# Turning the convolved channels token-major: transposes on TensorE in place of block transposes on VectorE and moves on ScalarE

## The reference

```python
xbc_act, conv_new = causal_conv(xbc, conv_prev, conv_w, conv_b)      # silu inside
xs, bm, cm = jnp.split(xbc_act, [SSD_WIDTH, SSD_WIDTH + SSD_GROUPS * SSD_STATE], axis=-1)
...
xdt = xr * dtr[..., None]
cb = jnp.einsum("bclgn,bcsgn->bcgls", cm, bm)
y_diag = jnp.einsum("bcgls,bcgrls,bcsgrp->bclgrp", cb, decay, xdt)
chunk_states = jnp.einsum("bcsgn,bcgrs,bcsgrp->bcgrpn", bm, decay_to_end, xdt)
...
y = y + xh.astype(jnp.float32) * d_skip.astype(jnp.float32)[:, None]
```

## Time and profile before

| | |
|---|---|
| median of 3 runs | 2809.83 us (2806.76 to 2810.88) |
| the profiled execution | 2810.88 us |
| its span, first to last instruction | 2809.1 us |
| mean granted TensorE clock | 0.992 |
| TensorE busy | 2760.9 us (98%) |
| VectorE busy | 1768.2 us (63%) |
| ScalarE busy | 1252.3 us (45%) |
| GpSimd busy | 824.4 us (29%) |

### The profile page before, as it was taken

The page is one execution under the profiler, slowest core; times in us unless marked ns, Lnnn a source line. Parts: engine busy times, 40 slices in busy tenths (PEclk is TensorE's granted clock), DMA queues, the critical chain, the costliest instruction groups (busy, mean ns, idle before and its releaser), DMA issues.

```text
span 2809.1 us, 38015 instructions
## 1 busy us (share of the span) xinstructions
PE 2760.9 (98%) x11971; PEld 1794.1 (64%) x11971; DVE 1768.2 (63%) x4770; ACT 1252.3 (45%) x2692; POOL 824.4 (29%) x1368
## 2 busy tenths in 40 slices
PE   8999999999999999999999999997999999999997
PEld 6776777777776777677777776773444444444443
DVE  5756666665666565656665656565666666666665
ACT  2334333343334333433343334334666666666665
POOL 1121112111211121111111121112556565555555
PEclk9999999999999999999999999998999999999999
DMA  7311111111111111111111111156888687778864
GB/s 309 146 46 53 61 68 46 53 61 68 46 49 65 67 47 46 68 54 61 46 63 58 61 46 56 38 195 226 317 296 293 233 277 252 280 266 286 316 218 146
DMA packets 104908, 377.88 MB, mean 135 GB/s; under 512 B 32713, under 2 KB 34642, under 8 KB 94706
## 3 DMA queue, kind: packets, MB, share of 16 engines
q1 hardware_dynamic: 44226, 236.13, 22.9%
q0 software_dynamic: 60480, 139.24, 14.7%
HBM read 326.14 MB, written 123.03 MB: 160 GB/s over the span
## 4 chain that ended last, share of the span: by engine, by line
PE 96%; DMA 2%; DVE 1%; ACT 1%; issue 1%; SPq 0%; POOL 0%; DVEq 0%; POOLq 0%; ACTq 0%
PE PB L367 25%; PE PB L1629 20%; PE PB L378 16%; PE PB L456 12%; PE SS L1648 5%; PE TB L1648 5%; PE YB L456 4%; PE YB L411 2%; PE TB L356 1%; DMA arena<-in_w_in 1%; PE SS L420 1%; PE TB L433 1%; PE SS L424 1%; PE YB L1639 1%; PE MB L402 1%
## 5 line engine op out<-in xcount | busy, mean ns | idle before, releaser
L367 PE MATMUL PB<-arena,hT 128*128 128x512 f32 (+2 forms) x2112 | 725.0, 496 | 1.5 <-ACT xT L590 0.8
L1629 PE MATMUL PB<-arena,hT 128*128 x1296 | 582.5, 592 | 0.0
L367 PEld LDWEIGHTS PB<-arena,hT 128*128 128x128 f32 x2112 | 396.8, 191 | 269.6 <-issue 222.6
L378 PE MATMUL PB<-hT,arena 128*128 128x128 f32 x4224 | 487.3, 276 | 3.7 <-DVE arena L1118 3.7
L378 PEld LDWEIGHTS PB<-hT,arena 128*128 128x128 f32 x4224 | 481.7, 193 | 7.8 <-issue 4.0
L1629 PEld LDWEIGHTS PB<-arena,hT 128*128 128x128 f32 x1296 | 239.9, 190 | 271.2 <-issue 271.2
L1155 POOL TENSOR_SCALAR rs<-sq 128x2 f32<-128x2 f32 (+1 forms) x66 | 14.2, 215 | 1284.4 <-ACT h L739 938.6
L456 PE MATMUL PB<-arena,tT 128*128 128x274 f32 (+1 forms) x1056 | 359.4, 495 | 0.7 <-ACT tT L634 0.7
L456 PEld LDWEIGHTS PB<-arena,tT 128*128 128x128 f32 x1056 | 196.1, 191 | 141.8 <-issue 121.5
L812 DVE SCALAR_TENSOR_TENSOR xc<-xT,cols,xc 128x128 f32<-128x128 f32 x792 | 216.8, 347 | 3.5
L1759 DVE TENSOR_TENSOR gv<-ycat,PB 128x256 f32<-128x256 f32 x81 | 34.1, 421 | 291.9 <-ACT ycat L1711 276.0
(11 more groups left out here) (288 smaller groups left out, 3990.0 us busy)
## 6 DMA issues: line engine op xcount, KB each, us to landing
arena<-in_w_expert SPq DMA_DIRECT2D x32, 2048.0 KB
arena<-in_w_expert SPq DMA_DIRECT2D x32, 1024.0 KB
h_rows<-h SPq DMA_DIRECT2D x34, 512.0 KB, 2.8
x_in<-in_x_rows SPq DMA_DIRECT2D x33, 512.0 KB, 4.4
hT<-in_x_cols SPq DMA_DIRECT2D x33, 512.0 KB, 3.5
x_res<-in_x_rows SPq DMA_DIRECT2D x33, 512.0 KB, 4.2
dec<-running_sums SPq DMA_DIRECT2D x33, 512.0 KB, 3.6
x_rows<-x_res SPq DMA_DIRECT2D x33, 512.0 KB, 2.6
```

Of the source, the lines that this page charges most:

```text
L367: mm = nc.tensor.matmul(out, hT[u][:, k, :], w_group(name)[:, k, :], start=k == 0, stop=k == KD - 1)
L378: mm = nc.tensor.matmul(PB[b][:, c * P:(c + 1) * P], w_block(name, c)[:, k, :], hT[u][:, k, :], start=k == 0, stop=k == KD - 1)
L1629: mm = nc.tensor.matmul(PB[u][:, :], hT[u][:, k, :], arena[:, bass.ds(slot + k * 2 * DE, 2 * DE)], start=k == 0, stop=k == KD - 1)
```

## The change

`xtok` and `btok` become two tensors. After projection z TensorE transposes the four x blocks into `TB[0]` and the two B blocks into `TB[1]`, and ScalarE copies both from there, between the SiLU of z and the exponentials. ScalarE's twelve moves and VectorE's six transposes go. The users of `TB` get waits on the new copies, `xb_out`, which now counts two per tile.

```diff
--- before.py
+++ after.py
@@ -181,8 +181,8 @@
         xT = [m[:, 0:CB * (P + HALO)].rearrange("p (b t) -> p b t", b=CB) for m in xT_mem]
         xT_s = xT_mem[0][:, :].rearrange("p (b q l) -> p b q l", b=CB, q=SB)
         xc = sb("xc", [P, CB, P])
-        xbtok = sb("xbtok", [P, W + G * N])
-        xtok, btok = xbtok[:, 0:W], xbtok[:, W:]
+        xtok = sb("xtok", [P, W])
+        btok = sb("btok", [P, G * N])
         gu = sb("gu", [P, W])
         zz = sb("zz", [P, W])
         gv2 = sb("gv2", [P, 2, W])
@@ -258,7 +258,7 @@
 
         names = """tail_packed xa_scaled w_scaled eout_a ws_ready wow_full wow_out xsq_ready xr_ready xi_ready rbc_full x_scaled
             proj_xa proj_xb proj_va proj_vb proj_u proj_z xa_out xb_evicted va_out gv_out gu_out z_out cache_set
-            halo_saved conv_done xc_ready cb_done xc_moved xb_out
+            halo_saved conv_done xc_ready cb_done xb_full xb_out
             dt_read lg_read cb_read rank_read dtneg_ready dtexp_ready dtrec_ready dt_ready acs_out sumT_done sumT_out
             ein_ready eout_ready seg_done decay_ready dec_ready xw_ready
             mixed_done bn_ready vr_ready v_ready ycat_hi
@@ -397,6 +397,11 @@
         def pe_front_channels(pe, t):
 
             pe.wait_ge(s["xc_ready"], t + 1)
+            after(pe, s["ycT_out"], 2 * t)
+            for b in range(2):
+                for k in range(4 - 2 * b):
+                    mm = nc.tensor.transpose(TB[b][:, k, :], xc[:, 4 * b + k, :], ident)
+                mm.then_inc(s["xb_full"], 1)
             pe.wait_ge(s["acs_out"], t + 1)
             for g in range(G):
                 mm = nc.tensor.matmul(cb_p[:, g * P:(g + 1) * P], xc[:, 4 + g, :], xc[:, 6 + g, :], start=True, stop=True)
@@ -427,6 +432,7 @@
         def pe_mix_pair(pe, i):
 
             pe.wait_ge(s["v_ready"], i + 2)
+            pe.wait_ge(s["xb_out"], 2 * i + 2)
             if i == 0:
                 pe.wait_ge(s["ws_ready"], 1)
             for h in range(H):
@@ -436,7 +442,7 @@
         def pe_mix_sample(pe):
 
             pe.wait_ge(s["v_ready"], NT)
-            pe.wait_ge(s["ycat_hi"], NP)
+            pe.wait_ge(s["xb_out"], 2 * NP + 1)
             pe.wait_ge(s["ws_ready"], 2)
             for h in range(H):
                 mm = nc.tensor.matmul(flat(TB[0][:, :, :])[:, h * HD:(h + 1) * HD], wsT_s[:, h, :], gv[0][:, h * HD:(h + 1) * HD],
@@ -446,7 +452,7 @@
         def pe_turned(pe, i):
 
             pe.wait_ge(s["ycat_ready"], i + 1)
-            transpose8(pe, block_of(ycat), lambda b: [("ycat_hi", i + 1)], "ycT_full")
+            transpose8(pe, block_of(ycat), lambda b: [("ycat_hi", i + 1)] if b == 0 else [("xb_out", 2 * i + 2)], "ycT_full")
 
         def pe_out(pe, i, b, free):
 
@@ -503,7 +509,7 @@
                 pe.wait_ge(s["w_scaled"], len(W_COLS))
             pe_out(pe, i, 0, (s["gu_out"], i + 2))
             if tn.next2:
-                pe_spread(pe, i + 2, TB[0], [("ycat_hi", i + 1)])
+                pe_spread(pe, i + 2, TB[0], [("xb_out", 2 * i + 3)])
             pe_out(pe, i, 1, (s["z_out"], i + 2))
             pe_out(pe, i, 2, (s["gated_ready"], i + 1))
 
@@ -578,8 +584,6 @@
 
 
 
-        channels_moved = [tmp[:, 0:192], tmp[:, 192:384], ycat[:, 0:192]]
-
         def act_channels(act, b, t, u, to_sample, done):
 
             if to_sample:
@@ -633,31 +637,22 @@
                 after(act, s["out2"], i)
                 nc.scalar.activation(tT[:, half(b), :], TB[b][:, :, :], ACT.Copy).then_inc(s["ycT_out"], 1)
 
-        def channels_quarter(g, q):
-            return xc[32 * g:32 * (g + 1), 0:6, 32 * q:32 * (q + 1)]
-
-        def act_move_channels(act, t):
-
-            act.wait_ge(s["xc_ready"], t + 1)
-            if t > 0:
-                act.wait_ge(s["ycat_hi"], t)
-                act.wait_ge(s["ycT_out"], 2 * t - 1)
-            for g in range(3):
-                for q in range(4):
-                    ins = nc.scalar.activation(channels_moved[g][32 * q:32 * (q + 1), :], channels_quarter(g, q), ACT.Copy)
-            ins.then_inc(s["xc_moved"], 1)
-
         def act_silu(act, t):
 
             act.wait_ge(s["conv_done"], t + 1)
             nc.scalar.activation(xc[:, :, :], xc[:, :, :], ACT.Silu).then_inc(s["xc_ready"], 1)
-            act_move_channels(act, t)
             act.wait_ge(s["proj_z"], t + 1)
             after(act, s["gated_ready"], t)
             nc.scalar.activation(zz[:, :], PB[1][:, :], ACT.Silu).then_inc(s["z_out"], 1)
 
         def act_front(act, t):
 
+            act.wait_ge(s["xb_full"], 2 * t + 1)
+            after(act, s["gated_ready"], t)
+            nc.scalar.activation(xtok[:, :], flat(TB[0][:, :, :]), ACT.Copy).then_inc(s["xb_out"], 1)
+            act.wait_ge(s["xb_full"], 2 * t + 2)
+            after(act, s["states_done"], t)
+            nc.scalar.activation(btok[:, :], flat(TB[1][:, 0:2, :]), ACT.Copy).then_inc(s["xb_out"], 1)
             act.wait_ge(s["ein_ready"], t + 1)
             act.wait_ge(s["state_ready"], t + 1)
             nc.scalar.activation(e_out[:, :], e_in[:, :], ACT.Exp).then_inc(s["eout_ready"], 1)
@@ -837,18 +832,10 @@
                 a = e_in[:, h:h + 1]
                 ins = V.tensor_scalar(dec[:, h, :], dec[:, h, :], a, a, ALU.min, ALU.subtract)
             ins.then_inc(s["seg_done"], 1)
-            by_token = xbtok[:, :].rearrange("p (c g i) -> p g c i", g=4, i=32)
-            dve.wait_ge(s["xc_ready"], t + 1)
-            after(dve, s["states_done"], t)
-            for q in range(4):
-                V.transpose(by_token[32 * q:32 * (q + 1), 3, :, :], channels_quarter(3, q))
             dve.wait_ge(s["cb_done"], t + 1)
             V.tensor_tensor(cbm[:, :, :], cb_p.rearrange("p (g t) -> p g t", g=G),
                             over(tri_s if t == NP else tri, G), ALU.mult).then_inc(s["cb_read"], 1)
-            dve.wait_ge(s["xc_moved"], t + 1)
-            V.transpose(by_token[:, 0:2, :, :], tmp[:, 0:384].rearrange("p (g c t) -> p g c t", g=2, t=32))
-            V.transpose(by_token[:, 2, :, :], ycat[:, 0:192].rearrange("p (c t) -> p c t", t=32)).then_inc(s["xb_out"], 1)
-            dve.wait_ge(s["xb_out"], t + 1)
+            dve.wait_ge(s["xb_out"], 2 * (t + 1))
             after(dve, s["ydiag_done"], t)
             st.inc(V.tensor_tensor(heads(xdt[:, :]), heads(xtok[:, :]), per_head(dt_t[:, :]), ALU.mult))
             after(dve, s["ysq_ready"], t)
```

## The result

The changed kernel takes 2829.39 us (median of 4 runs, 2827.98 to 2830.6), the kernel before 2809.76 in the same session (4 runs). The ratio is 1.0072, 95% interval 1.0054 to 1.0089: 0.7% slower, by 19.6 us. The profiled execution took 2827.62 us with a span of 2825.8, 16.7 us more than the span before.

What follows compares the result with a forecast made beforehand. TensorE, gapless in 32 turns, was taken to bound the kernel: 24.5 us for the transposes, less 1.0 for sample-turn waits and 3.5 for the clock, is 20.0 us more, so 2830 us, range 2826 to 2838.

Steps and rivals of the forecast that it cites:

- two terms of opposite sign: Six transposes in 32 gapless turns add 24.5 us; the sample turn saves 1.0 in waits and 3.5 in clock.
- What bounds: TensorE, 96% of the chain's span and gapless from 200 to 1800 us, pays nearly in full for added work.
- The six transposes: On TensorE between projection z and the C·B products: 0.77 us a tile, 24.5 us in 32 turns.
- the lower end: Six transposes at 0.112 us each, from four taking 0.45 us in the sample turn: 0.67 us a tile.
- Removed work worth nothing: In the 32 gapless turns, 4.4 us of ScalarE moves and 2.4 of VectorE transposes per tile save nothing.
- evictions hidden: ScalarE's copies of xtok and btok, 0.98 us together, finish with 6.9 us of cover before the spread transpose.
- The sample turn: TensorE's waits there, 0.65 us for cbm and 1.16 for dec, both go: 1.0 us less, six transposes included.
- The clock: Sample turn's fall to 0.50 goes with the pauses, saving 1.92 + 1.61 = 3.5 us; 6 in 10 on it.
- the dearer transpose: Rival: each new transpose runs as two pieces, 1.34 us a tile, 39 us in all, 2849; chance 0.05.
- the late copies: Rival: ScalarE's evictions outrun 6.9 us of cover; one us beyond in each turn is 32 us, 2862; chance 0.02.
- the hidden transposes: Rival: the six fit into TensorE's weight-load holes; at no cost the kernel is faster, 2805; chance 0.04.
- the clock did not fall in the gapless turns: Rival denied here: transposes lower TensorE's clock, 3.5 us in each of 33 turns, 116 us, 2950; chance 0.03.

Runs made afterwards that it cites:

- the transposes alone: Kernel before with the six transposes added on TensorE, results unread, old moves and block transposes kept: 2828.37 us against 2808.68, ratio 1.0069.
- the last experiment: Kernel before with the sample tile's new way, plus ycat's eight transposes moved off TensorE to ScalarE and VectorE for tiles 0 to 31: 2781.79 us, ratio 0.9910.
- Twelve in a row: Changed kernel with each of the six transposes made twice, twelve a tile: 2849.55 us, 21.9 more than the changed kernel's profiled execution.
- The 128 slices: Changed kernel with the copy of xtok cut into 128 copies of 4 columns on ScalarE: 2886.48 us, 58.9 more than the changed kernel's profiled execution.
- the sample tile's kernel: Kernel before with TensorE transposes and two ScalarE copies for the sample tile alone, old way for tiles 0 to 31: 2807.24 us against 2808.68, ratio 0.9996.
- the second profile: The kernel before, unchanged, profiled once more: 2812.21 us, single execution.
- 64 slices: Changed kernel with the copy of xtok cut into 64 copies of 8 columns on ScalarE: 2829.32 us.

## Why the prediction was right

The time was forecast at 2830 and is 2829.4. The mechanism was right; two terms of opposite sign were both too large, and that they cancel to within 1 us is luck.

**What bounds.** Right. TensorE stayed gapless and the transposes alone reproduce the whole slowdown.

**The six transposes: the term of the sum that was mis-sized.** I took 0.1275 us each from the eight of `ycat`, 24.5 us in 32 turns; they cost 0.66 a tile, 20.6 us in 31 turns and 0.66 more for tile 0, the lower end that I had from the four in the sample turn. The row that I chose had a neighbour's price in it: the last experiment shows that 0.15 to 0.19 of its 1.02 us are the price of the place behind the short matmuls. That it is a weight load left open fits the load records; no run took the short matmuls away. The new six stand behind projection z, whose long matmuls hide their first load: in turn 16 it starts at 971.32 us, 0.6 before z ends. Twelve in a row show that the price does not depend on the count.

**The rule on transposes in the Trainium skill** (TensorE: Matmul & The Clock Gate, Part 4: PE-mode transpose), about 275 ns inside a kernel, given there for bf16, agrees with the length of a record (0.273 us for the new ones) and not with the price, 0.11 us from one to the next. Its other statement, that transposes do not count as busy for the clock, changed nothing here: the granted clock is 1.00 with 9, 15 and 21 transposes a turn.

**Removed work worth nothing, evictions hidden.** Right: 6.7 us of cover against the 6.9 worked out. Over the whole program VectorE is busy 75 us less and ScalarE 118 (80 and 114 were forecast). The 128 slices show what lies beyond the cover: 1.34 us too late cost 1.59 a turn, in 31 turns, and not one for one in 32. The prediction looked for that price at the spread transpose alone; the first place to run out of cover is the sample turn, where 4.0 us of delay already made TensorE wait for `dec`.

**The sample turn.** Both waits went as worked out, and more: 8.85 us from z's end to ydiag became 7.53, 1.3 less and not 1.0. Of the other 0.3, 0.11 are the cheaper transposes and 0.17 the matmuls between, which take 7.04 us with the pauses among them and 6.87 without. The sums also came 1.2 us sooner in this profile, but the waits did not need it: the sample tile's kernel has the long way of the sums and the same 7.53. Nor is the change the only way to lose them: the transposes alone, with the short way of the sums, lose both waits as well.

**The clock.** In the two profiles 1.9 and 1.6 us came back, as forecast. In the timed runs the sample tile's new way brings 1.4 us of the expected 4.8, with no change inside the interval. I had priced the fall of a profiled execution as if it came in each; the second profile has it too, but by their times and mean clocks only some of the timed runs do. So 19.6 us between the medians are 33 x 0.66 = 21.8, less about 2, where the prediction's 20.0 were 24.5 less 4.5.

**The rivals.** Neither the dearer transpose nor the late copies nor the hidden transposes happened, and the clock did not fall in the gapless turns. For tile 0 it did fall in the changed kernel, at the new transposes (six took 0.91 us, the C·B products 0.85, the projection behind them 4.60 instead of 3.56), 1.7 us in all. Such a loss also comes without them: in the sample tile's kernel, which has none there, projection vb of turn 0 takes 5.70 us instead of 4.01. But six of the eight profiles with transposes for tile 0 have one of these two losses, and one of the four without. Whether the transposes make it likelier is open; what is at stake is 1.7 us.

## What to carry to other kernels

Where one engine is without a pause, price a change by what it adds to or takes from that engine, and look at the others only for their cover; here 83 and 122 us more on the two other engines bought 27, and 75 and 118 us less on them came with a loss of 20. Take the price of one more instruction from rows with the same neighbour: what stands before a short group decides whether its first weight load is hidden. A stall or a fallen clock in a profile is that execution's, so look at the spread and the mean clock of the timed runs before counting on its return. And where a total comes out as expected, set its parts beside the expectation too: the 59 us of the late copy were 49 and 10 in two places.

## What the runs showed of the hardware

- The clock did not follow the length of a pause. It fell behind a pause of 0.77 us (the kernel before, again), at the end of one of 1.16 that followed one of 0.65, 1.1 us behind one of 1.84 (64 slices), at the end of one of 2.47, and within one of 3.57, some 1.8 us after its start (128 slices). It did not fall behind one of 0.62, one of 0.82 (the last experiment, turn 0), nor behind any of 31 pauses of 1.34 us that stood a turn of 58 us apart. What tells these apart is open.
- Around tile 0's C·B products or in projection vb of turn 0 (5.70 us against 4.01) seven of the twelve profiles lose some 1.7 us of clock while TensorE is busy throughout. Neither profile of the kernel before does.
- ScalarE's small copies out of PSUM overlap: 64 of 128x8 in a row take 4.58 us, 0.072 from one to the next, though the record of one is 0.454 us long. 128 of 128x4 take 8.63 us and 32 of 128x16 take 2.56.
- A VectorE transpose on 32 partitions writes its blocks to other partitions than it reads: L844 reads partitions 96 to 127 and writes each quarter in turn, 0.37 us each for 32x192. So the sentence ahead of the prediction, that VectorE's transpose does not carry a block to other partitions, is too wide: it does not hold for those on 32 partitions, and so the fourth quarter gets to its place without a move.
